# Two blocks of a transformer in fp32 on one core: the down projection split over 8, 8 and 6 hidden tiles instead of 8, 6 and 8

## The reference

```python
D_MODEL, SEQ, D_FF = 1024, 512, 2816            # 2816 = 22 tiles of 128

def _swiglu(x, w_gate, w_up, w_down):
    return (jax.nn.silu(x @ w_gate) * (x @ w_up)) @ w_down

x = x + MACARON * _swiglu(_rmsnorm(x, ffn1_norm), w_gate, w_up, w_down)
```

```python
inv_freq = ROPE_BASE ** (-jnp.arange(0, QK_ROPE_DIM, 2) / QK_ROPE_DIM)
ang = positions[..., None] * inv_freq
return jnp.cos(ang), jnp.sin(ang)
```

## Time and profile before

| | |
|---|---|
| median of three runs | 3107.2 us (3106.8 to 3108.93) |
| profiled execution, its own time | 3106.85 us |
| its span in the profile | 3105.6 us |
| VectorE busy | 2168.9 us (70%) |
| ScalarE busy | 1624.8 us (52%) |
| GpSimd busy | 1650.7 us (53%) |
| DMA | 322.61 MB, mean 104 GB/s |

### The profile page before, as it was taken

The page is one execution under the profiler, slowest core; times in us unless marked ns, Lnnn a source line. Parts: engine busy times, 40 slices in busy tenths (PEclk is TensorE's granted clock), DMA queues, the critical chain, the costliest instruction groups (busy, mean ns, idle before and its releaser), DMA issues. The chain is left out here.

```text
span 3105.6 us, 52754 instructions
## 1 busy us (share of the span) xinstructions
PE 3080.5 (99%) x20424; PEld 2827.1 (91%) x20424; DVE 2168.9 (70%) x2975; ACT 1624.8 (52%) x2567; POOL 1650.7 (53%) x994
## 2 busy tenths in 40 slices
PE   9999999999999999999999999999999999999999
PEld 8999888999989998888999877889999788889998
DVE  8776467877668774577877578558775786478773
ACT  6555433555556554335555455556554575455553
POOL 5676433677657675434767433226676112257674
PEclk9999999999999999999999999999999999999999
DMA  4323322232322232322223232322232223323232
GB/s 141 113 103 123 120 76 75 102 110 109 123 86 105 109 117 102 113 82 82 109 107 112 93 95 82 118 93 106 99 122 105 95 93 121 114 89 109 109 110 82
DMA packets 93320, 322.61 MB, mean 104 GB/s; under 512 B 10512, under 2 KB 14992, under 8 KB 93072
## 3 DMA queue, kind: packets, MB, share of 16 engines
q1 hardware_dynamic: 87680, 312.07, 28.5%
q10 hardware_dynamic: 5392, 7.17, 0.7%
HBM read 316.05 MB, written 2.10 MB: 102 GB/s over the span
## 5 line engine op out<-in xcount | busy, mean ns | idle before, releaser
L3121 POOL TENSOR_TENSOR wlo<-raws,whi 128x1024 fp32r<-128x1024 f32 x369 | 891.8, 2420 | 1135.8 <-ACT whi L1218 884.4
L1218 ACT ACTIVATE whi<-raws 128x1024 fp32r<-128x1024 f32 x422 | 441.0, 1051 | 159.2 <-PE bank L505 57.2
L3129 POOL TENSOR_TENSOR f_s<-f_s,R 128x512 f32<-128x512 f32 x132 | 172.4, 1306 | 193.8 <-ACT f_s L1308 192.4
L640 PE MATMUL bank<-gxh,whi 128*128 128x256 f32 x1064 | 268.8, 283 | 1.2 <-ACT acc L1364 1.2
L641 PE MATMUL bank<-gxl,whi 128*128 128x256 f32 x1064 | 268.6, 283 | 0.0
L2219 DVE TENSOR_TENSOR wlo<-banks,whi 128x1024 fp32r<-128x1024 f32 (+1 forms) x166 | 196.9, 1186 | 68.9 <-ACT whi L1335 68.9
L640 PE MATMUL bank<-f_th,f_sh 128*128 128x256 f32 x944 | 236.9, 283 | 0.0
L641 PE MATMUL bank<-f_tl,whi 128*128 128x256 f32 x944 | 236.7, 283 | 0.0
L640 PE MATMUL bank<-f_th,whi 128*128 128x256 f32 x944 | 236.7, 283 | 0.0
L641 PE MATMUL bank<-f_tl,f_sh 128*128 128x256 f32 x944 | 236.7, 283 | 0.0
L501 PE MATMUL bank<-gxh,whi 128*128 128x512 f32 x584 | 229.9, 394 | 1.4 <-DVE gxl L2161 1.4
(11 more groups left out here) (597 smaller groups left out, 9192.7 us busy)
## 6 DMA issues: line engine op xcount, KB each, us to landing
raws<-stream SPq DMA_DIRECT2D x588, 512.0 KB, 3.3
xa_mem<-memT ACTq DMA_DIRECT2D x2, 1024.0 KB, 6.2
m_dk<-decay ACTq DMA_DIRECT2D x2, 514.0 KB, 4.5
x<-xT ACTq DMA_DIRECT2D x4, 256.0 KB, 5.3
x<-xT SPq DMA_DIRECT2D x4, 256.0 KB, 6.6
outT<-x SPq DMA_DIRECT2D x2, 512.0 KB, 3.0
m_ct<-cos ACTq DMA_DIRECT2D x2, 256.0 KB, 2.6
m_sn<-sin ACTq DMA_DIRECT2D x2, 256.0 KB, 2.9
```

Of the source, the lines that this page charges most:

```text
L640: pe.matmul(out, seq(hi, k, P), moving[k][0], start=first and k == 0, stop=False, skip_group_check=n != 1)
L1218: act.activation(M.whi[r][:, :], M.raw[r][:, :], ACT.Copy).then_inc(*S.tick("hi", u))
L3121: pool.tensor_tensor(M.wlo[r][:, :], M.raw[r][:, :], M.whi[r][:, :].bitcast(F32), ALU.subtract).then_inc(*S.tick("lo", u))
L3129: pool.tensor_tensor(T["s"][:, :], T["s"][:, :], M.R[:, :], ALU.mult).then_inc(*S.tick("silu_scaled", f, m))
```

## The change

It does four things.

1. `F_PARTS` becomes 8, 8 and 6 tiles, and `F_RUNS` 0 to 8, 9 to 16, 17 to 21. Part 2's steps have four blocks instead of three; part 3's units have 6 tiles instead of 8, and its first three units do 5 of them first and 1 later.
2. The 48 units of part 3 are loaded, rounded and subtracted at 768 columns instead of 1024.
3. Hidden tile 16 (before: 14), which is made ahead of part 2's steps and belongs to part 3, is rounded only in the step behind them, since all four odd buffers are in use until then. It stays unrounded in `u` for those four steps.
4. `rope_angles` and `decay_bounds` move from m = 1 of the residual stretch to VectorE's last step of seven products, behind the hidden tile of the step before and ahead of `first_row`; the load of the positions moves with the angles, and the tiles `rcos` and `rsin` lie 512 columns further.

```diff
-F_PARTS = ((0, 8), (8, 14), (14, 22))
-F_RUNS = ((0, 9), (9, 15), (15, 22))
+F_PARTS = ((0, 8), (8, 16), (16, 22))
+F_RUNS = ((0, 9), (9, 17), (17, 22))
...
+LAST = {U["down", f, 2, m] for f in range(6) for m in range(KD)}
+def unit_cols(u):
+    return (F_PARTS[2][1] - F_PARTS[2][0]) * P if u in LAST else UNIT
...
@@ tensor_program: last_tile, and part 3
-            for k in range(KD):
+            for k in range(len(pairs)):
...
-            part(("down", f, 2, m), banks[m][:, :], pairs, range(0, 6), True, False, arrive if m == 0 else None)
+            part(("down", f, 2, m), banks[m][:, :], pairs, range(0, len(ks) - 1), True, False, arrive if m == 0 else None)
...
-            part(("down", f, 2, m), banks[m][:, :], pairs, range(6, KD), False, True, arrive if m == 0 else None)
+            part(("down", f, 2, m), banks[m][:, :], pairs, range(len(ks) - 1, len(ks)), False, True, arrive if m == 0 else None)
...
@@ scalar_program
-        act.activation(M.whi[r][:, :], M.raw[r][:, :], ACT.Copy).then_inc(*S.tick("hi", u))
+        cols = unit_cols(u)
+        act.activation(M.whi[r][:, 0:cols], M.raw[r][:, 0:cols], ACT.Copy).then_inc(*S.tick("hi", u))
...
+            if after is None and i == M2_STAGE - 1:
+                act.wait_ge(*S.at("seven", f, s - 1, 4))
+                act.dma_start(M.m2["rsin"][:, :].bitcast(I32), T_in["pos"]).then_inc(*S.tick("pos2", by=16))
...
-            if before[0] == "tile":
+            if before[0] == "tile" and before[1] != PAIRED:
                 hidden_hi(before[1])
...
+            if SEQS[f][s] == ("tile", PAIRED + 1):
+                act.wait_ge(*S.at("seven", f, s - 1, 3))
+                hidden_hi(PAIRED)
...
@@ vector_program: residual, and step
-            if i == M2_STAGE - 1 and m == 1:
-                rope_angles()
-            if i == M3_STAGE - 1 and m == 1:
-                decay_bounds()
...
+            if not after and i == M2_STAGE - 1:
+                rope_angles()
+            if not after and i == M3_STAGE - 1:
+                dve.wait_ge(*S.at("seven", f, s - 1, 4))
+                decay_bounds()
             first_row(s)
...
@@ pool_program
+            if item == ("tile", PAIRED + 1):
+                hidden_lo(PAIRED)
+            if before[0] == "tile" and before[1] != PAIRED:
                 hidden_lo(before[1])
```

More of the change, by code:

```diff
@@ L328, in mixer2_tiles @@
                 ("pr0", 10 * P, F32), ("pr1", 10 * P, F32), ("pt0", 10 * P, F32), ("pt1_end", 2 * P, F32), ("ub0", SEQ + 16, F32), ("ub1", SEQ + 16, F32),
-                ("rcos", SEQ, F32), ("rsin", SEQ, F32), ("inv", 4 * 16, F32),
+                ("below_rcos", SEQ, F32), ("rcos", SEQ, F32), ("rsin", SEQ, F32), ("inv", 4 * 16, F32),
                 ("mx0", NB, F32), ("mx1", NB, F32), ("sums0", NB, F32), ("sums1", NB, F32), ("first", 16, F32)])
@@ L391, in hidden_tile @@
         k = m - PAIRED
-        name, k = ("odd", (k + 3) % 4) if k < 4 else ("tur0", k - 4)
+        name, k = ("odd", k) if k < 4 else ("tur0", k - 4)
         return seq(T[name + "h"], k), seq(T[name + "l"], k)
@@ L607, in last_tile @@
             pe.wait_ge(*S.at(*low_part(u)))
-            for k in range(KD):
-                mm = pe.matmul(b[:, 0:HALF], seq(lo, k, P), of_half(pairs[k][0], half), start=False, stop=k == KD - 1)
+            for k in range(len(pairs)):
+                mm = pe.matmul(b[:, 0:HALF], seq(lo, k, P), of_half(pairs[k][0], half), start=False,
+                               stop=k == len(pairs) - 1)
             mm.then_inc(*S.tick("last_half", half))
@@ L1246, in residual @@
             act.dma_start(M.m3["pos"][:, :], T_in["pos"]).then_inc(*S.tick("pos3", by=16))
-        if i == M2_STAGE - 1:
-            act.wait_ge(*S.at("hidden", 3, KF - 1))
-            act.dma_start(M.m2["rsin"][:, :].bitcast(I32), T_in["pos"]).then_inc(*S.tick("pos2", by=16))
         for m in range(KD):
@@ L3120, in lo @@
             return
-        pool.tensor_tensor(M.wlo[r][:, :], M.raw[r][:, :], M.whi[r][:, :].bitcast(F32), ALU.subtract).then_inc(
-            *S.tick("lo", u))
+        cols = unit_cols(u)
+        pool.tensor_tensor(M.wlo[r][:, 0:cols], M.raw[r][:, 0:cols], M.whi[r][:, 0:cols].bitcast(F32),
+                           ALU.subtract).then_inc(*S.tick("lo", u))
     def ffn(f):
@@ L3237, in sync_program @@
                 sp.wait_ge(*S.at("s13" if row == 2 else "s4", f, s))
-        sp.dma_start(M.raw[r][:, :], T_in["stream"][u]).then_inc(*S.tick(f"loaded{r}", u, by=16))
+        cols = unit_cols(u)
+        sp.dma_start(M.raw[r][:, 0:cols], T_in["stream"][u][:, 0:cols]).then_inc(*S.tick(f"loaded{r}", u, by=16))
         if u == U[("m2", 7)]:
@@ L3281, in tail_units @@
         if c == 2:
-            out.append(m_tiles(tiles[ks].reshape(UNIT, -1)))
+            rows = np.zeros((KD, *tiles.shape[1:]), w.dtype)
+            rows[0:b - a] = tiles[ks]
+            out.append(m_tiles(rows.reshape(UNIT, -1)))
             continue
```

## The result

The changed kernel takes 3115.8 us, median of 8 runs (3115.1 to 3117.5), against 3107.1 us of the kernel before in the same comparison: 1.0029 times, 95% interval 1.002 to 1.0038. It is 8.7 us slower. The profiled execution took 3115.41 us with a span of 3114.2.

What follows compares the result with a forecast made beforehand. TensorE bounds the kernel, busy 3080.5 of 3105.6 us. Terms -4.9 - 7.0 - 8.0 + 6.1 + 6.1 + 4.4 + 1.2 + 5.2 + 2.5 = +5.6 us on the profiled 3106.85 gave 3112.5 us, range 3100 to 3119.

Steps and rivals of the forecast that it cites:

- Parts 2 and 3, c22: All FFNs: matmuls +60.5 us in part 2, -65.4 in part 3; six TensorE waits for c22 go, -7.0.
- The angles leave the residual stretch: -8.0: FFN 4: TensorE's wait for a late rounding goes, 5.5 us, and the slow clock behind it, 2.5 us.
- The angles' new place: +5.2 and +2.5 of clock: End of FFN 4's last step: angles make c22 5.2 us late for the fourth product; slow clock adds 2.5.
- FFN 5: 6.1 given back: FFN 5's residual stretch: VectorE's chain bounds it, so of the shorter part 3's saving 6.1 us is lost.
- FFN 4: 4.4 given back: FFN 4's residual stretch: high half ends 42.1 us after part 3's start, unhindered TensorE 37.7; 4.4 us lost.
- FFN 2: 6.1 given back: FFN 2's residual stretch: VectorE keeps its own pace, so 4.8 of 10.9 us are gained and 6.1 lost.
- FFN 6: the end: FFN 6: only output 4's unit is late, 0.2 us given back in the halves at the end; net -1.9 us.
- 768 columns: Residual stretches: shorter GpSimd subtractions hold VectorE up less: 1.2 us in FFN 2, 2.0 in FFN 4, three times 0.55 in FFN 5.
- The wait "of over 4 us": FFN 5's residual stretch: one TensorE wait of over 4 us, for the unit whose rounding started at 2427.68.
- The gain stands: Rival: VectorE's stretches keep up with TensorE and the angles fit into the last step's pauses; 3087 us, chance 0.09.
- the angles don't: Rival: the stretches give back, but the angles' new wait stays under a microsecond, clock up; 3105 us, chance 0.15.
- slower, since the c22 waits stay: Rival: the waits in part 2's first step don't go, so the 7.0 us isn't gained; 3119.5 us, chance 0.16.
- The positions arrive late: Rival: in the last step VectorE stands still for the angles' late positions; time and chance counted in the slower case.

Runs made afterwards that it cites:

- e10: The changed kernel with the old parts (8, 6, 8) and 1024-column units in all six FFNs, angles and decay rates in VectorE's gaps: 3096.9 us.
- e6: The kernel before with only the angles and decay bounds moved to the last step, old parts and 1024-column units kept: 3106.7 us.
- e2: The changed kernel with the decay rates spread over VectorE's gaps, four operations per tile, and ScalarE's exponential ahead of the first x: 3111.1 us.
- e9: e7 with the old parts (8, 6, 8) and 1024-column units in FFN 2 and FFN 4: 3092.4 us.
- e7: The changed kernel with the decay rates in VectorE's gaps and the angles' twelve operations in three gaps (six, three, three): 3103.5 us.
- e4: The changed kernel with the 48 last units loaded, rounded and subtracted at 1024 columns again: 3124.3 us.
- e3: The changed kernel with the sums that turn x for FFN 3, in FFN 2's residual stretch, done on 8 of 256 columns: 3112.2 us.
- e11: The changed kernel with the 48 last units loaded and rounded on ScalarE at 1024 columns, subtracted on GpSimd at 768: 3117.1 us.

## Why the prediction came out as it did

The forecast was 3112.5 us and the result 3115.8, inside the range. (The +5.6 was added to the profiled execution; added to the median of the runs it is 3112.8.) The mechanism was right in every FFN. Three sizes were too small, mostly by the clock, and one was too large, so the sum came nearer than its terms.

- **Parts 2 and 3, c22.** FFN 1 was to gain 0.8 + 1.17 - 0.5 = 1.5 us and gained 1.3, FFN 3 the same. In FFN 1 the way to the start of part 3 is 8.9 us longer (84 more matmuls at 0.12, less the wait of 1.17), and part 3 takes 34.8 us instead of 45.0. Right, and e10 brings the six waits back.
- **The angles leave the residual stretch: -8.0.** e10 shows 7.9. Right.
- **The angles' new place: +5.2 and +2.5 of clock. Over-sized.** The wait was 4.35 us (4.5 with the modelled end). The angles took 9.0 us, 2.5 more than alone, where I had put 2.9 on the two meetings. (I let VectorE's operation end with GpSimd's; the row of 2.50 us ends 0.3 us after it.) Behind the wait the clock fell. e6 prices the place at 5.9 us in all instead of 7.7: the clock cost less than behind the old wait, since fewer matmuls ran slowly (0.86 instead of 0.79 over 12 us).
- **FFN 5: 6.1 given back.** Predicted T to high half 45.5 us, measured 45.2; net +4.1 and +3.7. Right, and e2 shows the chain to be the cause. The wait "of over 4 us" was 3.61; the slow matmuls behind it fell into waiting time, as said.
- **FFN 4: 4.4 given back. Mis-sized, and hidden by luck.** Net +2.1 and +1.8. e9 against e7 puts 3.8 us on it, net of the 2.0 (0.8 + 1.17) that the new parts gain in each FFN, so 5.8 were given back. The stretch from first x to last gxl was 29.0 us, as predicted (28.9). What the sum lacked is the clock behind the last wait of 2.18 us: 0.79 over 8 us, 1.7 us of time. It is about as large as the 1.8 by which the angles' place was over-sized.
- **FFN 2: 6.1 given back. Mis-sized.** 43.8 us were predicted and 44.7 measured from T to the high half. Of these 0.9 us 0.5 are in the chain (31.1 instead of 30.6, by the meeting at the last gxl), and 1.2 more came behind the high half. What I left out is the clock: it was put at nothing for FFN 2, but the last of its waits is 2.73 us long, and the clock fell behind it. The 98 matmuls of the next stage took 28.21 us instead of 22.26: 1.2 and 2.9 us for the two waits, and 1.9 for the clock. Net +6.1 instead of +4.1.
- **FFN 6: the end.** Net -0.6 instead of -1.9. In the window from 3100 to 3112 us the granted clock is 0.80; it fell 1.2 us after the end of a wait of 1.69 us and 1.9 us ahead of the last matmul, which at half the clock is 0.9 us. In the kernel before the same wait is there, and the clock fell only behind the last matmul. In 12 of the 14 traces here it fell ahead of it, and no run settles what decides. FFN 2 and 6 are 3.3 us; the other four came out 0.3 better together, and the rest of the difference to the 2.8 by which the whole was short is rounding and what lies ahead of the first cut.
- **768 columns.** I counted 1.2 us in FFN 2, 2.0 in FFN 4 and 1.7 in FFN 5 for meetings with GpSimd that go. Against the changed kernel e4 is longer by 1.7, 6.8 and 2.1 us there. FFN 4's price was under-sized. The stretch is 3.4 us longer there (32.4 instead of 29.0), 2.1 of it by the one tensor_scalar of line 2149; the wait for c22 is 0.7 us longer, and the granted clock is down behind it, behind a rounding that is 1.91 us late and behind the last gxl.
- **The rivals.** "The gain stands" fell by what FFN 2, 4 and 5 gave back, "the angles don't" by the 4.35 us wait, "slower, since the c22 waits stay" by their absence. "The positions arrive late" fell in the profiled execution by 0.02 us: in e2, e3 and e11, with the same code there, VectorE waited 1.3 to 1.6 us for them. The kernel is slower by over 0.2% all the same, by another way: the forecast's own terms, with more clock in them.

## What to carry to other kernels

Where a stage is covered by the one that feeds it, shorten the cover only where the follower has time left: read that stretch's chain from its first to its last instruction, and not the engine's share of the whole. The chain may run over two engines, and an engine's wait inside it (0.8 us a tile here) is room in which small independent work costs nothing. Where instructions of VectorE and GpSimd hold each other up, it counts which starts first and where it ends: 0.6 us of length on GpSimd was worth 6 us over 48 units, and 2 of them hung on one pair of instructions.
